# A two-block transformer kernel on one Trainium2 core: one more gate summed on VectorE, two gates' tiles held until behind the attention, and four edits in the router, the second attention and the last product

## The reference

```python
# block 1, modulation m = silu(c) @ w_ada in rows of 1024
h = modulate(rmsnorm(x), shift, scale)
y = token_mixer(h, h_ctx, ...)        # differential attention, 4 heads; HGRN2 scan, 4 heads; @ w_out
x = x + gate_1 * y
h = modulate(rmsnorm(x), shift2, scale2)
aff = softmax(h @ router)             # 16 experts; each takes its 32 strongest tokens
x = x + gate_2 * sum_e aff_e * (silu(h_e @ w_gate_e) * (h_e @ w_up_e)) @ w_down_e
# block 2, two layers, each: rmsnorm, modulate, layer, gate, residual
x = x + gate_3 * mla(h)               # latent attention, 8 heads
x = x + gate_4 * fourier(h)
return rmsnorm(x) * final_g
```

## Time and profile before

| what | value |
|---|---|
| time, median of 3 runs | 1067.82 us (1067.02 to 1069.67) |
| time of the profiled execution | 1067.25 us |
| its span | 1065.4 us |
| PE busy | 893.4 us (84%) |
| DVE busy | 390.1 us (37%) |
| ACT busy | 197.7 us (19%) |
| bytes moved | 310.19 MB, mean 291 GB/s |
| matmuls | 4378 |

### The profile page before, as it was taken

How to read it: one execution, slowest core, us unless ns; L and a number is a source line. 1 busy time by engine, 2 the same in 40 slices (tenths; PEclk the granted TensorE clock), 3 DMA queues, 4 the chain that set the end, 5 groups by cost and what they waited for, 6 DMA issues and landing times.

```text
span 1065.4 us, 11266 instructions
## 1 busy us (share of the span) xinstructions
PE 893.4 (84%) x4378; PEld 467.4 (44%) x4378; DVE 390.1 (37%) x689; ACT 197.7 (19%) x424; POOL 53.2 (5%) x128
## 2 busy tenths in 40 slices
PE   3999999999879698766666777676669999999997
PEld 2766565774644433222222222222225865644872
DVE  2199766679562511000000000000004484623232
ACT  2123321221452210000000000000004123411021
POOL 0200000000201100000000000000001100000000
PEclk9899999999999999888889888888889998999999
DMA  9973462644478799999999999999997785343300
GB/s 348 343 273 120 157 236 80 237 158 158 158 270 310 303 398 427 430 426 430 427 431 426 431 427 430 427 430 426 430 424 299 274 297 193 133 166 137 138 1 39
DMA packets 66774, 310.19 MB, mean 291 GB/s; under 512 B 2881, under 2 KB 5108, under 8 KB 53812
## 3 DMA queue, kind: packets, MB, share of 16 engines
q1 hardware_dynamic: 64276, 301.04, 70.8%
q0 software_dynamic: 2464, 8.68, 2.5%
HBM read 308.66 MB, written 1.05 MB: 291 GB/s over the span
## 4 chain that ended last, share of the span: by engine, by line
PE 58%; DMA 31%; DVE 5%; ACT 2%; issue 2%; SPq 1%; POOL 0%; POOLq 0%; DVEq 0%; ACTq 0%
PE bank L901 36%; DMA ring<-w_up_dram 28%; PE bank L1311 8%; PE bank L1605 3%; DMA ring<-w_in_dram 2%; DMA ring<-w_down_dram 2%; PE bank L1508 1%; PE bank L1066 1%; PE bank L920 1%; PE bank L1333 1%; PE bank L1514 1%; PE bank L1538 1%; ACT junk L1618 1%; PE bank L910 1%; DVE small L2337 1%
## 5 line engine op out<-in xcount | busy, mean ns | idle before, releaser
L1311 PE MATMUL bank<-ring,ilat 128*32 128x512 f32 x964 | 146.7, 762 | 106.3 <-DMA ring<-w_up_dram 105.3
L1311 PEld LDWEIGHTS bank<-ring,ilat 128*32 128x32 f32 x964 | 40.3, 135 | 209.3 <-issue 208.1
L2521 DVE TENSOR_TENSOR state<-state,bank 64x512 f32<-64x512 f32 x16 | 11.0, 690 | 304.5 <-ACT state L1865 304.5
L901 PE MATMUL bank<-ring,hT 128*128 128x512 f32 x224 | 97.1, 592 | 0.0
L901 PE MATMUL bank<-hT,ring 128*128 128x256 f32 (+1 forms) x320 | 88.9, 439 | 4.0 <-DVE hT L2063 2.0
L901 PE MATMUL bank<-ring,kT 128*128 128x512 f32 (+1 forms) x192 | 81.8, 583 | 0.0
L901 PEld LDWEIGHTS bank<-hT,ring 128*128 128x128 f32 x320 | 63.0, 199 | 28.4 <-issue 21.2
L1333 PE MATMUL bank<-ring,ilat 128*32 128x512 f32 x512 | 58.5, 595 | 14.9 <-ACT ilat L1869 12.5
L901 PEld LDWEIGHTS bank<-ring,hT 128*128 128x128 f32 x224 | 42.4, 190 | 52.6 <-issue 51.7
L1345 PE MATMUL bank<-state,ilat 128*128 128x512 f32 x128 | 57.7, 593 | 0.0
L1865 ACT ACTIVATE state<-bank 64x512 f32<-64x512 f32 x16 | 9.5, 591 | 255.1 <-PE bank L1311 255.1
(11 more groups left out here) (383 smaller groups left out, 1086.6 us busy)
## 6 DMA issues: line engine op xcount, KB each, us to landing
ring<-w_down_dram SPq DMA_DIRECT2D x30, 2048.0 KB, 23.6
ring<-w_up_dram SPq DMA_DIRECT2D x29, 2048.0 KB, 23.2
ring<-w_gate_dram SPq DMA_DIRECT2D x29, 2048.0 KB, 18.8
ring<-w_ada_dram SPq DMA_DIRECT2D x24, 2048.0 KB, 8.9
ring<-w_in_dram SPq DMA_DIRECT2D x8, 2048.0 KB, 13.9
ring<-fno_w_in_dram SPq DMA_DIRECT2D x4, 2048.0 KB, 10.4
ring<-w_out_dram SPq DMA_DIRECT2D x2, 2048.0 KB, 16.8
ring<-w_down_dram SPq DMA_DIRECT2D x4, 1024.0 KB, 10.0
```

The costliest lines, as they stand in the source:

```text
L901: ins = pe.matmul(o, l, r, start=start and i == 0, stop=stop and i == len(terms) - 1)
L1311: ins = pe.matmul(bank[0][32 * t:32 * t + 32, :], xin_cur[:, j, :], x[:, n0:n0 + TN], start=j == 0, stop=j == J - 1)
L2521: dve.tensor_tensor(hm, eg, bank[0][64:P, :], ALU.mult).then_inc(freed[0], 1)
```

## The change

Gate 11 is summed by DVE too. The sums of gates 10 and 11 are made behind the attention: gate 10's ahead of `head_out(1)`, gate 11's behind the router's scaled rows. Their products with ones stand between y(1, 0) and y(1, 1) of the out product, and their `gate_rows` behind the copy of shift_logits. The slots of both tiles are held until then, and the first expert's tiles for these slots are issued behind `extra_tile(6)`. The copy of the affinities goes: the first MAX8 and MATCH_REPLACE read the bank. Gate 16's sum goes into rounds 0 to 2 of the latent attention, gate 17's into rounds 3 to 6. ACT runs one exponential of one column ahead of the first of the latent attention. The last block of the last product is split into two of 256 columns, POOL adds the squares of the first two parts ahead, DVE multiplies by final_g before the root is there, and ACT scales the left and DVE the right half by it; the output goes out in four stores of 128 x 512.

```diff
--- before.py
+++ after.py
@@ -116,3 +116,4 @@
 LATER_GATES = GATE_MODS[4:]
-SUMMED_GATES = GATE_MODS[:3]
+SUMMED_GATES = GATE_MODS[:4]
+EARLY_GATES = 2
 
@@ -488,6 +489,4 @@
                     claim(("c2T",) + bg, 6 - b)
-                if n and GATE_MODS[n - 1] not in LATER_GATES:
-                    if GATE_MODS[n - 1] not in SUMMED_GATES:
-                        claim(("mod", GATE_MODS[n - 1]), 7)
-                    claim(("gt", GATE_MODS[n - 1]), 7)
+                if 0 < n <= EARLY_GATES:
+                    claim(("gt", SUMMED_GATES[n - 1]), 7)
                 if n in mix_work:
@@ -500,2 +499,4 @@
         claim(("shift_logits",), 5)
+        for k in range(EARLY_GATES, len(SUMMED_GATES)):
+            claim(("gt", SUMMED_GATES[k]), 4 + k)
         for b in range(TB):
@@ -518,2 +519,4 @@
 
+        last_blocks = [(0, 0, 0, TN), (0, 1, TN, TN), (1, 0, 0, TN), (1, 1, TN, T), (1, 2, TN + T, T)]
+
         def late_claims():
@@ -571,5 +574,4 @@
                 claim(("gt", LATER_GATES[2 + k]), 4 + k)
-            for b in range(TB):
-                for n in range(2):
-                    claim(("y3", b, n), 2 * b + n)
+            for b, n, _, _ in last_blocks:
+                claim(("y3", b, n), (2 * b + n, 6)[n // 2])
 
@@ -591,3 +593,3 @@
         rtmp = xbuf[1]
-        gate_sums = [tmpb[:, 0:TN], tmpb[:, D:D + TN], ebuf[1][:, 0:TN]]
+        gate_sums = [tmpb[:, 0:TN], tmpb[:, D:D + TN], qT[:, 0:TN], modr1[:, :]]
 
@@ -739,4 +741,3 @@
 
-            for _, s in first_slots[:2]:
-                first_tile(s)
+            held_longest = [slot_of["ada", i] for i in SUMMED_GATES[EARLY_GATES:]]
             wait_filled(sp, ("o", TB - 1))
@@ -745,3 +746,2 @@
             sp.wait_ge(sem("scratch_done"), 1)
-            wait_filled(sp, ("gt", SUMMED_GATES[-1]))
             first_half(EARLY_SLOTS, 2)
@@ -751,2 +751,5 @@
             extra_tile(6)
+            for s in held_longest:
+                first_tile(s)
+            assert [s for _, s in first_slots[:2]] == held_longest
             for _, s in first_slots[2:]:
@@ -792,6 +795,8 @@
             for b in range(TB):
-                sp.wait_ge(sem("result"), b + 1)
-                sp.dma_start(out[0].rearrange("(b p) d -> p b d", p=P)[:, b, :], xr3[:, b, :])\
-                  .then_inc(sem("stored"), 16)
-            sp.wait_ge(sem("stored"), 16 * TB)
+                for n, signal in enumerate(("left_result", "right_result")):
+                    cs = slice(n * TN, (n + 1) * TN)
+                    sp.wait_ge(sem(signal), b + 1)
+                    sp.dma_start(out[0].rearrange("(b p) d -> p b d", p=P)[:, b, cs], xr3[:, b, cs])\
+                      .then_inc(sem("stored"), 16)
+            sp.wait_ge(sem("stored"), 16 * 2 * TB)
 
@@ -803,3 +808,3 @@
 
-            def root_inverse(c0, n, signal, parts=None, eps=None):
+            def root_inverse(c0, n, signal, parts=None, eps=None, third=None):
 
@@ -810,4 +815,12 @@
                 rooted["last"] = ((signal, rooted[signal]),)
+                if third is not None:
+                    pool.wait_ge(sem("parts_squared"), 1)
+                    pool.tensor_scalar(meps[:, 1:2], ssq[:, parts:parts + 1], ssq[:, parts + 1:parts + 2], EPS,
+                                       ALU.add, ALU.add).then_inc(sem("mean_part"), 1)
+                    pool.wait_ge(sem("mean_part"), 1)
                 pool.wait_ge(sem("mean_square"), roots[0])
-                if eps is not None:
+                if third is not None:
+                    pool.tensor_tensor(meps[:, 0:n], meps[:, 1:2], ssq[:, third:third + 1], ALU.add)\
+                        .then_inc(sem("mean_eps"), 1)
+                elif eps is not None:
                     pool.tensor_tensor(meps[:, 0:n], ssq[:, c0:c0 + n], eps, ALU.add).then_inc(sem("mean_eps"), 1)
@@ -893,3 +906,3 @@
                 for b in range(TB):
-                    root_inverse(4 + b, 1, "rstd_x", 4 + 2 * b)
+                    root_inverse(4 + b, 1, "rstd_x", 4 + 2 * b, third=4 if k and b else None)
 
@@ -1182,4 +1195,4 @@
                     da_scores(*da[n + 2])
-                if n > 1 and GATE_MODS[n - 2] not in LATER_GATES:
-                    mod_gate(GATE_MODS[n - 2])
+                if 1 < n < EARLY_GATES + 2:
+                    mod_gate(SUMMED_GATES[n - 2])
                 wait_copied(pe, ("aT", b, h))
@@ -1195,4 +1208,2 @@
                     turn_chunks(("mixT", mix_work[n], 1), mix[:, mix_work[n], :], 1)
-                if n == len(SUMMED_GATES) + 1:
-                    mod_product(GATE_MODS[n - 1])
 
@@ -1225,2 +1236,5 @@
                     heads_product(1, n, g, g == 1, g == 0)
+                if n == 0:
+                    for k in range(EARLY_GATES, len(SUMMED_GATES)):
+                        mod_gate(SUMMED_GATES[k])
 
@@ -1598,4 +1612,4 @@
             for b in range(TB):
-                for n in range(2):
-                    w = wait_tile(pe, ("fout", n))
+                for n, c0, width in [x[1:] for x in last_blocks if x[0] == b]:
+                    w = wait_tile(pe, ("fout", c0 // TN))
                     o = pe_take(pe, ("y3", b, n))
@@ -1604,4 +1618,4 @@
                             pe.wait_ge(sem("mixed"), j // 2 + 1)
-                        ins = pe.matmul(o[:, :], oT3[:, j, b * P:(b + 1) * P], w[:, j, :],
-                                        start=j == 0, stop=j == J - 1)
+                        ins = pe.matmul(o[:, 0:width], oT3[:, j, b * P:(b + 1) * P],
+                                        w[:, j, c0 % TN:c0 % TN + width], start=j == 0, stop=j == J - 1)
                     fills(ins, ("y3", b, n))
@@ -1813,4 +1827,2 @@
                     take_mix(mix_work[n], 1)
-                if n == len(SUMMED_GATES) + 1:
-                    take_mod(GATE_MODS[n - 1])
             for b in range(TB):
@@ -1942,2 +1954,3 @@
 
+            st.did(act.activation(junk[:, 0:1], powers[:, 0:1], ACT.Exp))
             mla_exp(0)
@@ -1976,3 +1989,11 @@
             for b in range(TB):
-                residual_norm(3, b)
+                own = [x for x in last_blocks if x[0] == b]
+                for _, n, c0, width in own:
+                    act.wait_ge(sem("x_updated"), 2 * TB + 2 * b + n + 1)
+                    square(xr3[:, b, c0:c0 + width], (4 + 2 * b + n, 4)[n // 2], D,
+                           "mean_square" if n == len(own) - 1 else "parts_squared" if n else None)
+                act.wait_ge(sem("final_scaled"), 2 * b + len(own))
+                act.wait_ge(sem("rstd_x"), TB * 3 + b + 1)
+                st.did(act.activation(xr3[:, b, 0:TN], xn[:, b, 0:TN], ACT.Copy, scale=rr[:, 4 + b:5 + b]),
+                       sem("left_result"))
 
@@ -2278,4 +2299,4 @@
 
-            def gate_sum(k):
-                weighted_rows(SUMMED_GATES[k], gate_sums[k], "gate_sum")
+            def gate_sum(k, j0=0, j1=J):
+                weighted_rows(SUMMED_GATES[k], gate_sums[k], "gate_sum", j0, j1)
 
@@ -2286,4 +2307,2 @@
                 step(dve.tensor_scalar(c2[:, b, :], c2[:, b, :], rr[:, b:b + 1], None, ALU.mult), "c2_normed")
-            gate_sum(2)
-
 
@@ -2391,2 +2410,3 @@
                         take_context(b_, g)
+            gate_sum(2)
             head_out(1)
@@ -2435,2 +2455,3 @@
                  "router_scaled")
+            gate_sum(3)
 
@@ -2444,2 +2465,4 @@
             frees(st, dve.tensor_copy(shift_logits, o[:, 0:E]), ("shift_logits",))
+            for k in range(EARLY_GATES, len(SUMMED_GATES)):
+                gate_rows(k)
             add_normed("y", 0, 1, lambda: take_turned(0))
@@ -2467,9 +2490,8 @@
             o = wait_filled(dve, ("affT",))
-            frees(st, dve.tensor_copy(affT, o[0:E, 0:T]), ("affT",))
-            st.settle()
             for r in range(CAP // 8):
-                src = affT if r == 0 else work
+                src = work if r else o[0:E, 0:T]
                 step(dve.max(top8, src))
                 st.settle()
-                step(dve.match_replace(work, top8, src, -1.0))
+                ins = dve.match_replace(work, top8, src, -1.0)
+                step(ins) if r else frees(st, ins, ("affT",))
                 st.settle()
@@ -2596,3 +2618,2 @@
             late_product(3)
-            weighted_rows(LATER_GATES[0], late_gate_sums[0], "late_gate")
             for b in range(TB):
@@ -2627,2 +2648,4 @@
 
+            gate_rows_in = [((0, 0, 5),), ((0, 5, 6),), ((0, 6, 8),), ((1, 0, 2),), ((1, 2, 4),), ((1, 4, 6),),
+                            ((1, 6, 8),), ()]
             mla_max(0)
@@ -2644,4 +2667,4 @@
                     mla_max(k + 2)
-                if 1 <= k <= 4:
-                    weighted_rows(LATER_GATES[1], late_gate_sums[1], "late_gate", 2 * k - 2, 2 * k)
+                for i, j0, j1 in gate_rows_in[k]:
+                    weighted_rows(LATER_GATES[i], late_gate_sums[i], "late_gate", j0, j1)
                 if b == 0 and m:
@@ -2682,6 +2705,14 @@
             for b in range(TB):
-                add_branch("y3", 3, b)
```

(13 more changed lines are left out.)

## The result

The changed kernel took 1057.76 us (median of 4 runs, 1056.82 to 1058.83), the kernel before 1068.74 (4 runs) beside it: a ratio of 0.9901, 95% interval 0.9887 to 0.9916, so 9 to 12 us faster. Forecast were 1061.4 us, a range of 1058.8 to 1064.0, and 6.45 us of gain.

The account below looks back on a forecast made before the run. The weight stream bounds 378 to 789 us, PE mostly the stretches before and behind. Terms -0.35 (to the first expert product), -4.9 and -1.2 sum to -6.45: 1067.25 becomes 1060.8, plus 0.57 gives 1061.4 us; range 1058.8 to 1064.0.

Parts of the forecast that it names:

- Gate 10 out of the stretch ahead of the attention, 0: Ahead of the attention: eight DVE instructions go, but PE runs a gapless block of 10.03 us over them; 0.
- Attention, -1.6: Attention: pair 5's turn starts 1.6 us sooner without the wait for gate 10's bank; nothing more for gate 11's selection matmul.
- bound of -3.0: Attention: the far end of its term, -3.0 us, if removing gate 11's selection matmul counts as well.
- Rival (a): Attention: PE's thinner work brings another 3.4 us stretch at the lower clock, costing 1.7 us: 1063.1 us; chance 0.14.
- Out product, +1.7, and the affinities, -0.45: Out product: two gates' rows of ones add 1.7 us on PE; router: dropping the affinities' copy saves 0.45.
- The held tiles, 0: Out product and router: the stream absorbs 4.19 MB in room for 5.5 MB, so 0; +9.8 us as other end.
- rival (d): Expert stage: the moved transfers aren't absorbed and it ends up to 9.8 us later: 1071.2 us; chance 0.05.
- Latent attention, -5.5 + 0.6 = -4.9: Latent attention: PE's 2.76 us wait and the clock's fall behind it go, -5.5; DVE late in round 6, +0.6.
- the second fall: Latent attention: clock at 0.50 from 890.5 to 893.9 us behind 32 small two-column matmuls; assumed to stay.
- rival (b): Latent attention: no clock fall behind the small matmuls, giving back 1.7 us: 1059.7 us; chance 0.12.
- Early table load, 0: Latent attention: ACT's 1.28 us table load for the exponential moves early; PE has small matmuls over it, 0.
- Tail, -1.2: Behind the last product: smaller evictions -0.54, square -0.2, split final product -0.65, store +0.2; -1.2 us.

Follow-up runs that it names:

- filler_att: Kernel before plus two products of 512 columns, results unused, in PE's idle ahead of the values of pair 6: 1064.8 us, ratio 0.9986.
- aff: Kernel before with only the first MAX8 and MATCH_REPLACE reading the affinities from their bank: 1066.73 us, ratio 0.9989.
- gates: Kernel before with only gates 10 and 11 both summed by DVE behind the attention, their tiles held: 1065.57 us, ratio 0.9977.
- no_gates: Changed kernel without its part on gates 10 and 11: 1062.66 us, ratio 0.9953 to the kernel before.
- best: Changed kernel with gate 10 as before, gate 11 alone held and moved, and gated_out first in round 6 of the latent attention: 1060.52 us, ratio 0.9928.
- better: Changed kernel with gate 10 summed ahead of the attention, its product in round 6, gate_rows behind, and gated_out first in latent round 6: 1057.93 us, ratio 0.9918.
- control: Kernel before, unchanged, timed against itself: 1067.81 us, ratio 1.0004.
- tail: Kernel before with only the split last product and the four stores: 1067.46 us, ratio 0.9995.
- the four comparisons: Changed kernel against the kernel before, first and three later on other chips: ratios 0.9901, 0.9917, 0.9913, 0.9923; mean 0.9914, 9.2 us.
- mla: Kernel before with only gates 16 and 17 summed inside the rounds of the latent attention: 1064.54 us, ratio 0.9963.
- swap: Changed kernel with gated_out ahead of gate 17's last two rows in round 6 of the latent attention: 1056.15 us, ratio 0.9901; again 1057.15, 0.9928.
- after3: Changed kernel as it is, run again beside the kernel before: 1057.84 us, ratio 0.9913.

## Why the prediction was wrong

Step by step, with the mean over traces where several show a stage:

- *Gate 10 out of the stretch ahead of the attention, 0*: right. The start of the attention scatters by 3 us, and not with this edit.
- *Attention, -1.6*: mis-sized; -3.25 measured, just beyond the bound of -3.0. What I had worked out came: the turn of pair 5 stands 8.08 us behind pair 4's before, 6.49 after, -1.6. Nothing more for the selection matmul was right too. Without it the turn of pair 6 comes 3.05 us behind instead of 3.94, but the values of pair 6, for which the chain waits, stand 6.76 us behind the turn of pair 5 before and 6.74 after; PE only waits 0.86 longer (3.08 for 2.22 us), for a copy that stands on ACT behind pair 7's exponentials (rows below; 310.55 and 313.26 us in the trace of after). The missing 1.65 stand behind these values, where the stretch at 0.52 was: 6.76 us to the first product with w_out before, 5.11 after, and 5.12 in `filler_att`, whose code from these values on is the one of before. Rival (a), a further fall from thinner work, had the wrong sign here: the fall that was there went away, and where one came earlier in three traces it cost nothing. The attention's length is the same with gate 11 alone.
- *Out product, +1.7, and the affinities, -0.45*: together +1.25 forecast, +1.68 measured. `aff` has -0.54, `gates` +2.13: the row of both gates costs its 1.72, and 0.26 is a longer stretch at the lower clock in the router (from PE's turn of qT, L1265, to the first expert product 7.23 us in `gates`, 6.97 before).
- *The held tiles, 0*: right. Arguing from room (5.5 MB for 4.19) held, and rival (d) had 0.05.
- *Experts, not a term*: -0.9 in the trace of after, and 0.8 to 1.0 in the other six traces of kernels with both gates moved behind the attention (427.17 to 427.36 us). It is the least certain term: without that part `no_gates` has 426.56 and `best` 430.25 us. In these two traces the wait for the last tile ends as much behind the first expert product as before (419.4 against 419.5 us), in others not (418.7 in `no_gates`, 420.5 in `better`). What is shorter is the last gate and up product, 5.26 us against 6.10, which runs at the lower clock for less long.
- *Latent attention, -5.5 + 0.6 = -4.9*: the wait and the first fall were right against this trace (PE at the first small products 6.05 us sooner, 0.5 of it from before the stage), and round 6 gave +0.8 for 0.6. But that the fall costs 2.75 us was the reading of one execution: the same two groups take 1.3 us less in `control` and `tail`, and lose nothing in two other traces. I took the second fall to stay, and gave rival (b), in which it goes, 0.12. It went, in every trace of this kernel. In the eight traces of the old order the stage holds 3.4 to 10.2 us at the lower clock, mean 7.7; half of that, 3.8, and the wait of 2.8 less 0.8 in round 6 is 5.8, an estimate. Against their mean the stage gained 5.6, against the trace that I had read, 6.6.
- *Early table load, 0*: right, shown alone.
- *Tail, -1.2*: right, -1.27. In it the store: two issues of 0.81 us together instead of one of 0.36, and 2.2 instead of 2.6 us of landing, by the profile's list of issues. The formula that the prediction takes from the Trainium skill ("DMA: Bandwidth & Descriptors", section "Anatomy of one DMA") is given there for transfers that GpSimd issues; these stores are SyncE's.

The rows to the attention, of before and of after:

```profile
306.88 0.66 PE L1142 MATMUL bank<-const,gates 128*128 128x128 f32 x4
...
310.26 0.69 ACT L1766 ACTIVATE gates<-bank,small 128x512 f32<-128x512 f32 x1 [2.09 <-DVE small L2340]
...
310.82 0.60 PE L1142 MATMUL bank<-const,gates 128*128 128x128 f32 x4
...
312.97 0.62 ACT L1771 ACTIVATE gates<-bank 128x512 f32<-128x512 f32 x1
```

```profile
307.20 0.63 PE L1155 MATMUL bank<-const,gates 128*128 128x128 f32 x4 [1.94 <-ACT smat L1807]
...
310.25 0.60 PE L1155 MATMUL bank<-const,gates 128*128 128x128 f32 x4
```

The sum of measured stages, with the mean for the latent attention, is -3.25 + 1.68 - 0.9 - 5.6 - 1.27 = -9.3, against 9.2 from the four comparisons: nothing is missing from it. The step that failed is that the clock's falls were taken as a fixed part of each stage, one kept in the attention, one kept in the latent attention, a further one added as a rival. The runs showed in its place that they come and go with the change: 1.65 us in the attention, 0.7 in the mean of the latent attention and 0.9 in the last expert are clock, and 0.3 the other way in the router. That the clock accounts for the time is shown by the traces; what makes it fall or stay in the latent attention and the last expert is not.

The range also failed on its own terms: it stopped at 1058.8 with the second fall's 1.7 in it, and the bound of -3.0 for the attention, which I had worked out, was left out of it.

## What to carry to other kernels

An instruction taken off an engine is worth its time only as far as the next wait: the wait for gate 10's bank ahead of a turn was worth its 1.6 us, the selection matmul behind it nothing, since the next product waited for ACT by as much longer. Follow the path through the order from mark to mark and don't stop at the first instruction that comes sooner. When a wait of TensorE is removed, price the slow stretch behind it together with the wait, put its disappearance and its staying into the range as two values of one term, and read its size from more than one execution. Compare stages from mark to mark over several executions; one trace's absolute times moved by 3 us here for no reason in the code, and a kernel rebuilt from the better stages (`best`) was not faster.

## What the runs showed of the hardware

- Useless products in a gap of 2.2 us went with a full clock behind it (2.08 became 1.16 us), and the attention became 1.6 us shorter by added work; without them all eight traces have the fall. A gap of 3.08 us at the same place of another kernel had no fall behind it. In a gap of 2.8 us of the latent attention a filler showed nothing, since two of eight traces without one have no fall right behind the gap either.
- Whether a fall occurs repeats from run to run for some places (the stretch behind the attention: all eight traces with gate 11 in it and no filler there, 44.5 to 44.8 us behind the first scores, though these start anywhere from 268.0 to 270.2 us) and not for others (797 to 808 us: three traces of twenty; latent attention of one and the same order: 54.98 to 58.29 us).
- A fall needs no gap: in `mla` PE is busy in every window from 878 to 893 us, and the clock is 0.86 and 0.57 in two of them.
- A fall can be free: in three traces with gate 11 moved (better, swap, after3) PE has 0.83 to 0.86 from 300 to 310 us, and the attention is 48.07 to 48.16 us long against 48.03 to 48.06. Eight products take 2.07 instead of 1.16 us there (`after3`), and the wait behind them is 1.50 instead of 3.08.
- MAX8 of 16 x 256 takes 0.42 us from PSUM and from SBUF alike.
- A 512 KB store split in two of 256 KB lands 2.2 us behind its issue instead of 2.6.
